# Staggering the first four weight slots of a two-block model kernel by 32 bytes each

## The chip, the core and the metric

One core of a Trainium2 chip runs the whole program. TensorE (PE) multiplies, VectorE (DVE) and ScalarE (ACT) do elementwise work, GpSimd (POOL) does a little of it, and SyncE (SP) issues the weight transfers. The metric is device time in microseconds for one execution. The kernel before takes 2011.96 us, the median of three runs (2011.53 to 2012.35).

## The reference

The input is 256 tokens by 1024 features, batch 1, all in float32. The reference computes one block of a first kind and two of a second, in a row:

```python
def swiglu(y, w_in, w_out):
    a, b = jnp.split(y @ w_in, 2, axis=-1)
    return (jax.nn.silu(a) * b) @ w_out
...
x = ada_out(x, swiglu(ada_in(x, mod, 0, ...), ffn_w_in[l, 0], ffn_w_out[l, 0]), ...)   # also for ctx
# first block: a bidirectional chunked recurrence and a pooling mixer on w_in (1024 x 2064), w_out
x = ada_out(x, swiglu(ada_in(x, mod, 2, ...), ffn_w_in[l, 1], ffn_w_out[l, 1]), ...)
...
for l in range(2):   # second block
    x = x + 0.5 * rms_norm(swiglu_ffn(h, gate, up, down), ...)      # 1024 x 2816 twice, 2816 x 1024
    x = x + rms_norm(hybrid_mixer(h, w_in[l], ...), ...)            # 1024 x 7184, attention, conv, GLA
    x = x + 0.5 * rms_norm(swiglu_ffn(h, gate, up, down), ...)
```

Nearly all arithmetic is products of 256 tokens (512 with the context, in the first block) with large float32 weights. Each weight is read once.

## The kernel before

**Split products.** TensorE's fast float32 form (`float32r`) rounds its operands. So each operand is split into a rounded part and a remainder, hi and lo, and each product is three: hi x hi, hi x lo, lo x hi. In the class Tensor, `product` (L971, L972, L973) streams the weight part as the moving operand, 512 columns, against token parts loaded as stationary weights of the array; in the trace these are `bank<-whi,xTh`, `bank<-wlo,xTh` and `bank<-whi,xTl`, with other token tiles in the place of xTh and xTl. `sub_w` (all through the helper at L935) loads the weight part as stationary and streams 256 tokens: `bank<-xTh,whi` and its like.

**The weight stream.** SP copies a unit of weights (512 KB or 1024 KB) into one of the four raw buffers of `raw`. A unit is cut into sub-units of 128 partitions x 1024 floats. For each sub-unit ACT copies raw to `whi` with rounding (`fill` of Scalar, L1562; L1572 where a gain per row is multiplied in, two instructions of 512 each), then DVE writes raw minus whi to `wlo` (`fill` of Vector, L2191; L2202 with the gain), then TensorE uses both. A slot is one pair whi, wlo, 4096 bytes each per partition. There are 23 slots; slots 0 to 3 are always in the ring, the others borrow memory that is free in some stage (Tables.place deals the slots). All waits between engines are semaphores, and the order on every engine is fixed when the program is written.

**Where the tiles lie.** `Memory.place` gives every tile an address per partition, one after another: raw at 16544, then whi0, wlo0, whi1, ... wlo3, then x, z, junk and the rest. The first address is 160 modulo 256, and nearly all sizes are multiples of 256, so raw, all 23 slots, xTh, xTl, the hidden tiles (hTh, hTl, hwh, hwl), x, z and junk all begin at 160 modulo 256. A few begin elsewhere: modr and brow at 0, yT at 224, sg, qT, kT, mg and tm at 32, gv at 64. uC's rows are 1144 bytes, so its reads begin at many places. Reading through columns of a slot or of xTh moves by multiples of 512 bytes, so an instruction begins where its tile does.

Of the kernel before, what the change touches and what calls it, by code (L numbers as in the profile page):

```python
# [7 lines left out]
F32R = mybir.dt.float32r  # L8
# [83 lines left out]
class Tables:  # L92
# [16 lines left out]
    def place(self):  # L109

        q = len(self.subs)
        s = min(self.ring, key=lambda s: self.guard[s][3] if s in self.guard else -1 if self.holder[s] is None else self.holder[s])
        p, extra = None if s in self.guard else self.holder[s], None
        if s in self.guard:
            kind, key, due, _ = self.guard.pop(s)
            if kind == "spent":
                p = key
            else:
                extra = (kind, key)
            self.due.append(max(self.due[-1] if self.due else 0, due))  # L120
        else:
            self.due.append(max(self.due[-1] if self.due else 0, 0 if p is None else p + 2))
        self.slot.append(s)
        self.before.append((p, extra))
        self.holder[s] = q
        if s in self.once:
            self.ring.remove(s)
            self.once.remove(s)
# [362 lines left out]
class Memory:  # L491
# [47 lines left out]
    def place(self):  # L539
        o = self.low  # L540
        self.raw, o = self.at(o, "raw", [128, NRAW, 2048])
        self.wh, self.wl = [None] * NSPL, [None] * NSPL
        for n in range(4):
            o = self.split_slot(n, o)
        self.x, o = self.at(o, "x", [128, 2, D])
        self.z_at = o
        self.z, o = self.at(o, "z", [128, 2, D])
        self.junk_at = o
        self.junk, o = self.at(o, "junk", [128, D])
        self.ident, o = self.at(o, "ident", [128, 128])  # L550
        self.cols, o = self.at(o, "cols", [128, NCOL + 2])
        self.stats, o = self.at(o, "stats", [128, 24, 8])
        self.fullb, xt = self.at(o, "full", [128, 2, 512])
        self.xTh, o = self.at(xt, "xTh", [128, 8, 256], F32R)
        self.xTl, mid = self.at(o, "xTl", [128, 8, 256], F32R)
        self.bT, o = [], mid
        for n in range(3):
            self.split_slot(4 + n, o)
            if n == 1:
                self.b1_at = o  # L560
            h, o = self.at(o, f"bT{n}h", [128, 4, 256], F32R)
            l, o = self.at(o, f"bT{n}l", [128, 4, 256], F32R)
            self.bT.append((h, l))
        self.xc, o = self.at(xt + 32768, "xc", [128, 2, D])
        self.gp, o = self.at(o, "gp", [128, 2, D])
        self.modc, o = self.at(o, "modc", [128, 3, 2, 2, 8])
        self.gcol, o = self.at(o, "gcol", [128, 3, 2, 8])
        self.selm, o = self.at(o, "selm", [128, 258])
        self.modr, o = self.at(o, "modr", [128, 2, 512])
        self.brow, o = self.at(o, "brow", [128, 2, 512])  # L570
        self.sct, ctx = self.at(o, "sct", [128, 8, 32])
        ctx += (xt - ctx) % 256
        self.place_first(xt, mid, ctx)
        self.place_context(mid)
        self.place_latent(xt, mid)
        gate = xt + 45056
        self.split_slot(7, gate + 4096)
        self.split_slot(8, gate + 12288)
        self.gate, rest = self.at(gate, "gate", [128, 6, 2, 512])
        sil, o = self.at(gate, "silb", [128, 4, 256])  # L580
        self.ffn = {1: self.place_ffn(ctx, "a"), 2: (*self.place_ffn(rest - 4096, "b")[:4], sil)}
        for n, o in ((12, ctx), (15, rest - 4096)):
            self.split_slot(n, o + 2 * HALF_H)
            self.split_slot(n + 1, o)
            self.split_slot(n + 2, o + HALF_H)
        for n in range(5):
            self.split_slot(18 + n, rest + 8192 * n)
        self.place_mixer(rest)

    def split_slot(self, n, o):  # L590
        self.wh[n], o = self.at(o, f"whi{n}", [128, 1024], F32R)
        self.wl[n], o = self.at(o, f"wlo{n}", [128, 1024], F32R)
        return o
    def place_first(self, xt, mid, o):
        self.cTh, c = self.at(mid, "cTh", [128, 8, 256], F32R)
        self.cTl, c = self.at(c, "cTl", [128, 8, 256], F32R)
        assert c == mid + 16384
        self.h = h = o
        self.hwh, o = self.at(o, "hwh", [128, 22, 256], F32R)
        self.hwl, o = self.at(o, "hwl", [128, 22, 256], F32R)  # L600
        self.zc = self.at(o - 8192, "zc", [128, 2, D])[0]
        self.hx, f = self.at(o, "hx", [128, 2, 512])
        self.silx, self.top = self.at(f, "silx", [128, 2, 512])
        self.wh[9], self.wl[9] = self.at(o, "whi9", [128, 1024], F32R)[0], self.at(f, "wlo9", [128, 1024], F32R)[0]
        self.split_slot(10, h)
        self.split_slot(11, h + 22528)

    def place_context(self, mid):

        o = self.top  # L610
        self.vac, o = self.at(o, "vac", [128, 2, 4, 129])
        self.wk, o = self.at(o, "wk", [128, 4, 128])
        self.gb, o = self.at(o, "gb", [64, 2])
        o = mid + 16384
        self.mst, o = self.at(o, "mst", [64, 12])
        self.ones, self.xc_rest = self.at(o, "ones", [64, 128])
        self.uPc, o = self.at(self.xc_rest, "uPc", [128, 4, 258])
        self.g16c, o = self.at(o, "g16c", [128, 256])
        self.Cc, o = self.at(o, "Cc", [128, 2, 64])
        assert o <= mid + 16384 + 8192  # L620
        self.Rc, o = self.at(mid, "Rc", [64, 7, 256])
        self.S0, o = self.at(o, "S0", [128, 8, 129])
        self.S1, o = self.at(o, "S1", [128, 8, 129])
        assert o <= mid + 16384
        self.ktc, o = self.at(self.z_at, "ktc", [128, 2, 512])
        self.uc, o = self.at(o, "uc", [128, 4, 256])
        self.kvc = self.at(self.xc_rest, "kvc", [128, 8, 129])[0]
# [2516 lines left out]
```

How the kernel before makes its waits and increments, by code:

```python
    def __init__(self, m, e):  # L715
        for u, sources in enumerate(m.t.units):
            if u - NRAW in m.t.mod_read:
                nb, half, count = m.t.mod_read[u - NRAW]
                b, n = m.t.bank["mod", nb]
                if half:
                    e.wait_ge(m.full[b], n + 1)
                else:
                    e.wait_ge(m.mod_half, count)
            elif u - NRAW in m.t.part_read:
                e.wait_ge(m.part_done, m.t.part_read[u - NRAW])
            elif u >= NRAW:
                e.wait_ge(m.wlo_done, m.t.subs_through[u - NRAW])
            raw = m.raw[:, u % NRAW, :]
            for part, n, src in sources:
                if part in (0, 1):
                    dst = raw.rearrange("p (k j n) -> p k j n", k=4, j=2)[:, :, part, :]
                else:
                    dst = raw[:, part].rearrange("p (k n) -> p k n", k=n)
                e.dma_start(dst, src).then_inc(m.raw_in[u % NRAW], 16)
        new = 2 * (4 + 2 + 2 + 2 * 6)
        e.wait_ge(m.x_new, new - 2)
        e.dma_start(m.out[0:128, :], m.x[:, 0, :]).then_inc(m.stored, 16)
        for half in range(2):
            c = slice(half * 512, half * 512 + 512)
            e.wait_ge(m.x_new, new - 1 + half)
            e.dma_start(m.out[128:256, c], m.x[:, 1, c]).then_inc(m.stored, 16)
        e.wait_ge(m.stored, 48)
# [5 lines left out]
    def __init__(self, m, e):  # L748
# [25 lines left out]
            if k == 17:  # L774
                e.wait_ge(m.conv1, 8)
                e.wait_ge(m.po_act, 2)
                for n in range(2):
```

## Time and profile before

| | us |
|---|---|
| three runs, median | 2011.96 |
| the profiled execution, its own time | 2011.67 |
| its span, first to last instruction | 2009.5 |
| PE busy in the span | 1978.9 |
| DVE busy | 1343.7 |
| ACT busy | 1106.1 |

The granted TensorE clock is 0.999 of full speed over the span. A matmul's recorded time is longer than the distance to the next one, since two are in the pipeline at once; the distance from start to start is what a product costs.

### The profile page before, as it was taken

How to read it: one execution, taken by the hardware profiler on the slowest of the kernel's cores; microseconds unless marked ns; L12 is line 12 of the kernel's file. 1: busy time of each engine (PE TensorE's matmuls, PEld its weight loads, DVE VectorE, ACT ScalarE, POOL GpSimd, SP SyncE). 2: the span in 40 equal slices, each digit the busy share in tenths (PEclk: the TensorE clock that was granted, in tenths of full speed). 3: DMA queues.
4: the chain of work that ended last, by engine and by line, in shares of the span. 5: the costliest groups of instructions: out<-in, count | busy, mean ns of one | idle time of the engine just before them, and what ended most of it. 6: DMA issues, size and time to landing. Idle time of an engine off the chain costs nothing.

```text
span 2009.5 us, 27521 instructions
## 1 busy us (share of the span) xinstructions
PE 1978.9 (98%) x10838; PEld 1680.9 (84%) x10838; DVE 1343.7 (67%) x2184; ACT 1106.1 (55%) x1746; POOL 70.2 (3%) x139
## 2 busy tenths in 40 slices
PE   7999999999999999999999999999999999999998
PEld 5998899987778888888997888888888897788887
DVE  4457676675887556655688896646665587987653
ACT  4344465445674445554656756545555646766552
POOL 0000000001100000000100000000000200000000
PEclk9999999999999999999999999999999999999999
DMA  9797755675377656555643476555656544367551
GB/s 338 254 303 256 245 190 173 215 255 183 124 233 251 199 195 214 179 196 180 201 147 105 148 238 211 189 168 179 218 174 214 191 126 158 126 203 227 188 185 46
DMA packets 282175, 393.23 MB, mean 196 GB/s; under 512 B 9660, under 2 KB 175996, under 8 KB 282048
## 3 DMA queue, kind: packets, MB, share of 16 engines
q1 hardware_dynamic: 277616, 379.62, 57.5%
q0 software_dynamic: 3456, 9.37, 1.4%
q10 hardware_dynamic: 976, 2.49, 0.3%
q8 instruction: 86, 1.41, 0.3%
q14 instruction: 41, 0.34, 0.1%
HBM read 390.40 MB, written 1.05 MB: 195 GB/s over the span
## 4 chain that ended last, share of the span: by engine, by line
PE 85%; DVE 7%; ACT 3%; DMA 2%; issue 2%; SPq 0%; POOL 0%; DVEq 0%; POOLq 0%; ACTq 0%
PE bank L971 21%; PE bank L973 21%; PE bank L972 21%; PE bank L935 20%; DMA raw<-in_ffn_w_in 2%; DVE wlo L2191 1%; PE bank L1112 1%; DVE junk L2916 1%; PE bank L1020 1%; ACT whi L1562 1%; DMA raw<-in_w_mod 1%; DVE wlo L2202 1%; ACT whi L1572 1%; DVE tm L3073 0%; SPq L734 0%
## 5 line engine op out<-in xcount | busy, mean ns | idle before, releaser
L2191 DVE TENSOR_TENSOR wlo<-raw,whi 128x1024 fp32r<-128x1024 f32 x358 | 433.4, 1224 | 277.0 <-ACT whi L1562 271.2
L1562 ACT ACTIVATE whi<-raw 128x1024 fp32r<-128x1024 f32 x360 | 375.7, 1055 | 376.0 <-PE bank L973 218.0
L971 PE MATMUL bank<-whi,xTh 128*128 128x512 f32 (+1 forms) x1344 | 528.8, 393 | 2.4 <-DVE xTl L2265 2.3
L973 PE MATMUL bank<-whi,xTl 128*128 128x512 f32 (+1 forms) x1344 | 520.7, 387 | 0.0
L972 PE MATMUL bank<-wlo,xTh 128*128 128x512 f32 (+1 forms) x1344 | 520.0, 387 | 0.0
L2202 DVE SCALAR_TENSOR_TENSOR wlo<-raw,cols,whi 128x512 fp32r<-128x512 f32 (+1 forms) x592 | 403.0, 733 | 149.0 <-ACT whi L1572 145.6
L1572 ACT ACTIVATE whi<-raw,cols 128x512 fp32r<-128x512 f32 (+1 forms) x592 | 380.5, 704 | 142.9 <-PE bank L973 108.2
L971 PEld LDWEIGHTS bank<-whi,xTh 128*128 128x128 f32 x1344 | 252.6, 188 | 54.9 <-DVE xTl L2265 3.1
L973 PEld LDWEIGHTS bank<-whi,xTl 128*128 128x128 f32 x1344 | 252.4, 188 | 52.2
L972 PEld LDWEIGHTS bank<-wlo,xTh 128*128 128x128 f32 x1344 | 252.8, 188 | 49.0 <-issue 0.5
L935 PE MATMUL bank<-xTh,whi 128*128 128x256 f32 x696 | 197.0, 284 | 0.0
L935 PE MATMUL bank<-xTl,whi 128*128 128x256 f32 x696 | 195.9, 283 | 0.0
L935 PE MATMUL bank<-xTh,wlo 128*128 128x256 f32 x672 | 190.1, 283 | 0.0
L971 PE MATMUL bank<-whi,hThb 128*128 128x512 f32 x352 | 138.0, 392 | 0.0
L973 PE MATMUL bank<-whi,hTlb 128*128 128x512 f32 x352 | 137.1, 389 | 0.0
L972 PE MATMUL bank<-wlo,hThb 128*128 128x512 f32 x352 | 137.0, 389 | 0.0
L935 PEld LDWEIGHTS bank<-xTh,whi 128*128 128x128 f32 x696 | 133.5, 192 | 1.3 <-issue 1.0
L935 PEld LDWEIGHTS bank<-xTl,whi 128*128 128x128 f32 x696 | 133.5, 192 | 0.4 <-issue 0.2
L935 PEld LDWEIGHTS bank<-xTh,wlo 128*128 128x128 f32 x672 | 128.9, 192 | 0.0
L935 PE MATMUL bank<-cTh,whi 128*128 128x256 f32 x392 | 112.1, 287 | 1.0 <-DVE wlo L2191 0.7
L935 PE MATMUL bank<-cTl,whi 128*128 128x256 f32 x392 | 110.6, 283 | 0.0
L935 PE MATMUL bank<-cTh,wlo 128*128 128x256 f32 x384 | 108.6, 283 | 0.0
(381 smaller groups left out, 2439.2 us busy)
## 6 DMA issues: line engine op xcount, KB each, us to landing
raw<-in_w_in SPq DMA_DIRECT2D x68, 1024.0 KB, 5.1
raw<-in_ffn_w_in SPq DMA_DIRECT2D x132, 512.0 KB, 5.7
raw<-in_ffn_w_gate SPq DMA_DIRECT2D x88, 512.0 KB, 4.1
raw<-in_ffn_w_up SPq DMA_DIRECT2D x88, 512.0 KB, 5.1
raw<-in_ffn_w_down SPq DMA_DIRECT2D x40, 1024.0 KB, 5.0
raw<-in_w_mod SPq DMA_DIRECT2D x36, 1024.0 KB, 6.0
raw<-in_ffn_w_out SPq DMA_DIRECT2D x30, 1024.0 KB, 5.6
raw<-in_w_out SPq DMA_DIRECT2D x12, 1024.0 KB, 5.1
```

Of the source, the lines that this page charges most:

```text
L935: return self.e.matmul(o, lhsT, rhs, start=start, stop=stop, skip_group_check=True)
L971: e.matmul(o, hi[:, kc, sl], wh[:, c], start=at == 0 and k == 0, stop=False)
L972: e.matmul(o, hi[:, kc, sl], wl[:, c], start=False, stop=False)
L973: ins = e.matmul(o, lo[:, kc, sl], wh[:, c], start=False, stop=fin)
L1020: ins = self.e.transpose(bank[:, c * 128:c * 128 + 128], src[:, k * 128:k * 128 + 128], self.m.ident[:, :])
L1112: ins = e.transpose(bank[:, (2 * c + i) * 128:(2 * c + i + 1) * 128], htok[:, 2 * (g % 2) + i, c * 128:c * 128 + 128], m.ident[:, :])
L1562: e.activation(wh, raw, ACT.Copy).then_inc(m.whi_done, 1)
L1572: ins = e.activation(wh[:, c], raw[:, c], ACT.Copy, scale=m.cols[:, a + k:a + k + 1])
L2191: e.tensor_tensor(wl, raw, wh.bitcast(F32), ALU.subtract).then_inc(m.wlo_done, 1)
L2202: ins = e.scalar_tensor_tensor(out=wl[:, c], in0=raw[:, c], scalar=m.cols[:, a + k:a + k + 1], in1=wh[:, c].bitcast(F32), op0=ALU.mult, op ...
L2916: ins = e.scalar_tensor_tensor(out=y[:, c, :], in0=m.uC[:, c, j:j + 256], scalar=w_, in1=y[:, c, :], op0=ALU.mult, op1=ALU.add)
```

## The change

Between whi0 and wlo0, wlo0 and whi1, and so on to wlo3, 32 bytes are left free. So wlo0 begins 32 bytes further on, whi1 64 bytes, and wlo3 224 bytes; modulo 256 the eight parts begin at 160, 192, 224, 0, 32, 64, 96 and 128. x and everything after it lies 256 bytes further on, so that its place modulo 256 is as before. That makes the memory 256 bytes too short at its end, so the small tile gb (two gate biases, 8 bytes per partition) moves from the end into a hole behind sct.

```diff
         for n in range(4):
-            o = self.split_slot(n, o)
+            o = self.split_slot(n, o, 32)
...
-        self.sct, ctx = self.at(o, "sct", [128, 8, 32])
+        self.sct, o = self.at(o, "sct", [128, 8, 32])
+        self.gb, ctx = self.at(o, "gb", [64, 2])
         ctx += (xt - ctx) % 256
...
-    def split_slot(self, n, o):
+    def split_slot(self, n, o, gap=0):
         self.wh[n], o = self.at(o, f"whi{n}", [128, 1024], F32R)
-        self.wl[n], o = self.at(o, f"wlo{n}", [128, 1024], F32R)
-        return o
+        self.wl[n], o = self.at(o + gap, f"wlo{n}", [128, 1024], F32R)
+        return o + gap
...
         self.wk, o = self.at(o, "wk", [128, 4, 128])
-        self.gb, o = self.at(o, "gb", [64, 2])
```

No instruction is added, removed or moved: on each of the five engines the order, the operands' names and the semaphores are the same. Only the line numbers differ: from L613 on a line is numbered two higher, so L971 becomes L973, L1562 becomes L1564 and L2191 becomes L2193.

Of the 9448 product matmuls of the program, counted in its list of instructions, 6460 read slots 0 to 3: 3612 with 512 moving columns and 2848 with 256. ACT has 968 rounding instructions and DVE as many for the remainders; 607 of each write slots 0 to 3.

## Rows read from the trace of the kernel before

**Rows 1.** The page: busy us (share of the span) x instructions, by engine.
```profile
PE 1978.9 (98%) x10838; PEld 1680.9 (84%) x10838; DVE 1343.7 (67%) x2184; ACT 1106.1 (55%) x1746; POOL 70.2 (3%) x139
```

**Rows 2.** Waits of PE: engine, line, releaser: us in total, times, longest us.
```profile
PE bank L935 <- DMA raw<-in_w_mod: 11.5, 3, 6.9
...
PE bank L935 <- DVE wlo L2191: 0.7, 2, 0.4
```

**Rows 3.** The page: lines' shares of the chain that ended last.
```profile
PE bank L971 21%; PE bank L973 21%; PE bank L972 21%; PE bank L935 20%; DMA raw<-in_ffn_w_in 2%; DVE wlo L2191 1%; PE bank L1112 1%; DVE junk L2916 1%; PE bank L1020 1%; ACT whi L1562 1%; DMA raw<-in_w_mod 1%; DVE wlo L2202 1%; ACT whi L1572 1%; DVE tm L3073 0%; SPq L734 0%
```

**Rows 4.** The chain in order of time: start us, us, what (longest pieces).
```profile
277.76 1.75 PE bank L1020 x16
...
351.37 51.59 PE bank L935 x432
976.15 46.07 PE bank L935 x384
```

**Rows 5.** Windows: stretch, length, busy us of PE, PEld, DVE, ACT, POOL; clock, DMA.
```profile
1022.22:1033.13 10.91, 10.91 (x51) 9.02 (x50) 10.91 (x32) 7.75 (x20) 0.00 (x0) 1.00 0.35 104
829.94:834.02 4.08, 4.08 (x19) 3.38 (x19) 1.82 (x3) 2.32 (x4) 0.00 (x0) 1.00 0.78 240
```

**Rows 6.** Windows, the same columns: two groups of an FFN.
```profile
834.30:857.02 22.72, 22.72 (x105) 18.81 (x104) 14.01 (x24) 13.12 (x22) 0.00 (x0) 1.00 0.58 186
```

**Rows 7.** Timeline of PE, mixer: start us, us, instruction; junk begins at 160.
```profile
1115.22 1.89 PE L935 MATMUL bank<-junk,stk 128*128 128x256 f32 x8
1116.76 0.58 PE L971 MATMUL bank<-whi,xTh 128*128 128x512 f32 x1
```

**Rows 8.** Timeline of PE, same mixer: sg begins at 32.
```profile
1128.74 1.89 PE L935 MATMUL bank<-sg,stk 128*128 128x256 f32 x8
1130.27 0.58 PE L971 MATMUL bank<-whi,xTh 128*128 128x512 f32 x1
```

**Rows 9.** Timeline of PE, x8 transposes of x (160), then slower products.
```profile
1205.67 1.04 PE L1020 MATMUL bank<-ident,x 128*128 128x128 f32 x8
1206.46 0.47 PE L971 MATMUL bank<-whi,xTh 128*128 128x512 f32 x1
...
1207.00 0.40 PE L973 MATMUL bank<-whi,xTl 128*128 128x512 f32 x1
...
1208.39 0.40 PE L973 MATMUL bank<-whi,xTl 128*128 128x512 f32 x1
```

**Rows 10.** Timeline of PE, x8 transposes of mg (32).
```profile
1797.90 1.04 PE L1497 MATMUL bank<-ident,mg 128*128 128x128 f32 x8
1798.69 0.48 PE L971 MATMUL bank<-whi,xTh 128*128 128x512 f32 x1
```

**Rows 11.** Groups by shape: line, instruction, count; busy us, mean ns; idle before.
```profile
L2191 DVE TENSOR_TENSOR wlo<-raw,whi 128x1024 fp32r<-128x1024 f32 x358 | 433.4, 1224 | 277.0 <-ACT whi L1562 271.2 <-POOL stats L855 3.7
L1562 ACT ACTIVATE whi<-raw 128x1024 fp32r<-128x1024 f32 x358 | 374.5, 1058 | 373.9 <-PE bank L973 215.9 <-PE bank L935 85.2 <-DMA raw<-in_ffn_w_in 57.7
L2202 DVE SCALAR_TENSOR_TENSOR wlo<-raw,cols,whi 128x512 fp32r<-128x512 f32 x560 | 389.6, 747 | 145.1 <-ACT whi L1572 141.7
```

**Rows 12.** Instructions of L2265: ns min/median/max, first and last start us.
```profile
L2265 DVE TENSOR_TENSOR hwl<-hx,hwh x22: 683/684/693, 57.3 to 405.2; 128x512 fp32r<-128x512 f32 x22
L2265 DVE TENSOR_TENSOR xTl<-yT,xTh x2: 671/672/672, 543.6 to 545.0; 128x512 fp32r<-128x512 f32 x2
```

**Rows 13.** Instructions on the tiles modr, mg and junk, the same columns.
```profile
L2359 DVE SCALAR_TENSOR_TENSOR modr<-raw,sct,modr x42: 743/752/755, 174.2 to 653.8; 128x512 f32<-128x512 f32 x42
L3075 DVE TENSOR_TENSOR mg<-mg,tm x16: 691/692/694, 1160.1 to 1795.9; 128x512 f32<-128x512 f32 x16
L2110 ACT ACTIVATE sg<-junk x2: 1061/1062/1064, 1121.5 to 1740.0; 128x1024 f32<-128x1024 f32 x2
```

**Rows 14.** Instructions on the tile gb: the DMA, and ns of one reader.
```profile
L2634 DVE TENSOR_SCALAR Rx<-bank,gb x2: 466/469/472, 501.3 to 502.3; 32x256 f32<-32x256 f32 x2
L762 POOL DMA_DIRECT2D gb<-in_gate_b x1: 552/552/552, 160.2 to 160.2; - x1
```

## The prediction

> **What bounds the kernel now.** I read the busy shares first. PE is busy 1978.9 of 2009.5 us, 98%, with DVE at 67% and ACT at 55% [rows 1]. The page warns that a busy PE is not a PE at its peak, so I went on to PE's own waits. The longest is for a DMA at the very start, 11.5 us; for the remainders (wlo), which the changed addresses touch, PE stood still 0.7 us in the whole span [rows 2]. The chain of waits says the same: the three 512-column products have 21% each and the 256-column ones 20%, together 83%; the two kinds of remainder instruction and the two kinds of rounding come to about 1% each [rows 3]. So the kernel is as long as TensorE's stream of products, and the change can move the time only if it changes the distance between two products, or makes a product wait for a rounded or a remainder part.
>
> Next I took that distance in stretches of one kind. 432 products with 256 columns take 51.59 us and 384 others 46.07 us: 0.119 and 0.120 us each [rows 4]. With 512 columns, 18 starts lie in 4.08 us, 0.2267 us each, while DVE is busy less than half and ACT a little more than half of the stretch. In another stretch, where DVE is busy the whole time and ACT for 7.75 of 10.91 us, 48 starts lie in 10.91 us, 0.2273 us each [rows 5]. (The counts in those rows include the matmuls cut by the edges.) At the granted clock 1.00, which is the 2.4 GHz level, 512 columns are 0.2133 us, so 0.013 us of each product is something else.
>
> **The change, part by part.**
>
> *The products themselves.* 6460 of 9448 product matmuls read slots 0 to 3. Before, the streamed operand and the loaded one both begin at 160 modulo 256. Afterwards the distance between the two is one of eight values, from 0 to 224. The question is whether a matmul, or a matmul beside DVE and ACT, notices that. The trace has no split product with unequal beginnings, so I take the nearest rows. Eight matmuls of 256 columns stream junk, which begins at 160; the next instruction starts 1.54 us after them [rows 7]. Eight of the same form in the same mixer stream sg, which begins at 32, against the same small matrix: 1.53 us [rows 8]. That is 0.192 us for each, whether the beginning is 160 or 32. Eight transposes of x (160) take 0.79 us to the next start and eight of mg (32) also 0.79 us [rows 9, 10]. In both pairs the difference is under 0.01 us in eight, about 1 ns for one. The value is 0. The bounds from the same rows are 1 ns either way, for 6460 products 6.5 us. That is the last digit of the view filled to its edge, so I allow half of it, 3.2 us, for this term.
>
> *The products beside DVE and ACT.* If three engines at the same place modulo 256 got in each other's way, it would show where they overlap. It shows 0.6 ns (0.2273 against 0.2267) between the stretch where DVE never rests and the one where it mostly does [rows 5]. For 3612 products with 512 columns in slots 0 to 3 that is at most 2.2 us, if the whole of it were a matter of beginnings and the stagger removed all of it. I take 0: the engines move through their operands at different rates, so where each begins says little about where they stand against each other a moment later.
>
> *Remainders and rounding.* DVE reads raw and whi and writes wlo in step, one element each at a time, so here a common beginning could count. A remainder takes 1224 ns and a rounding 1058 ns for 1024 elements, one with a gain 747 ns for 512 [rows 11]. For unequal beginnings there are rows: the same subtraction of 512 elements takes 684 ns in the middle with all three tiles at 160, and 672 ns with the source (yT) at 224 [rows 12], 12 ns or 1.8% less. The scalar-tensor form with raw at 160 and its other input and its output (modr) at 0, just as a staggered slot would stand, takes 752 ns, 5 ns more than the 747; the sum of two tiles at 32 takes 692 ns, 8 ns or 1.2% more than 684; and ACT from junk (160) to sg (32) takes 1062 ns against 1058 [rows 11 to 13]. So one instruction changes by between -1.8% and +1.2%, and the row that is nearest to a staggered slot says +0.7%. These four kinds hold about 4% of the chain, 80 us [rows 3], and 607 of 968 of them are in the slots concerned: 50 us of the path, so -0.9 to +0.6 us. I take 0, since the rows of both signs are equally near. Off the path a few nanoseconds do nothing: DVE waited 271 us for ACT's rounding [rows 11], and TensorE's 0.7 us is all that it waited for DVE in turn. If that cover were gone, all 607 would count, at 5 ns each 3 us.
>
> *The rest.* x, z, xTh and all later tiles move by 256 bytes and keep their place modulo 256: 0. gb moves, is loaded once by one small DMA, and is read by eight DVE instructions of about 470 ns [rows 14]: at most a few ns each, 0. raw doesn't move, so no weight transfer changes its target. No instruction, wait or queue entry changes, so nothing is queued behind anything new.
>
> The sum is 2011.67 us (the profiled execution, 2009.5 of it the span) + 0 + 0 + 0 = 2011.7 us. The median of the three runs is 0.29 us higher, 2011.96. I forecast 2011.9 us. The allowances, 3.2, 2.2 and 0.9 us, seldom add up; together they make about 3 us each way.
>
> **A rule weighed.** Rows 5 say 0.6 ns between a crowded and a less crowded stretch. The Trainium skill, in "SBUF — State Buffer", section "A bandwidth-pool intuition that's wrong (but worth ruling out)", says that the memory is multi-ported and that contention on it is structural, a lock on a port or a starved descriptor generator, and no sharing of one bandwidth; the section "Door 1: The DMA port swizzle" of the same page puts the banks that the compute engines see in groups of partitions, not in addresses along a partition. By that rule the stagger has nothing to act on, and the sum is exactly that of before; the trace agrees to within the 0.6 ns that it leaves.
>
> **The rivals.**
>
> *Faster: collisions of address go away.* Two groups of a feed-forward stage take 22.72 us for 96 products and 8 transposes [rows 6]. 96 x 0.2267 is 21.76 us, and 8 transposes at 1.75/16 = 0.109 us [rows 4] are 0.88 us, together 22.64. Some 0.08 us, 0.35%, is left, and one sees it as products at longer distances: from 1207.00 to 1208.39 us six take 1.39 us, 0.232 us each, 5 ns more than the usual [rows 9]. If that excess were collisions of equal beginnings throughout, it would be 0.35% of 2009.5 us, 7.1 us, and the share of slots 0 to 3 is 6460/9448 of it, 4.8 us: 2007.1 us. For it: the excess exists, and everything stands at 160 now. Against it: it lies in the few products after transposes, and the busiest stretch for DVE lacks it [rows 5]. A larger form would attack the 13 ns that a product takes over its columns; 6460 times that is 84 us, for which only the number speaks, since it is the same for the streams of 256 and of 512 columns and looks like a fixed cost of changing the stationary operand.
>
> *Slower: the stagger makes collisions.* It could be that equal beginnings are the good case for TensorE's two reads, since the streamed and the loaded operand then keep a fixed distance, and that some of the seven new distances make them meet. The place is the 512-column stream on slots 0 to 3, the price the one slow distance that the trace knows, 5 ns [rows 9]: 3612 x 5 ns = 18 us, 2030 us; if half of the distances do it, 9 us, 2021 us. It decides from 1.1 ns per product (4 us / 3612). For it: no product of the trace has unequal beginnings. Against it: junk against sg, and x against mg, show no difference for such a pair [rows 7 to 10].
>
> *The change doesn't do what it says.* The places modulo 256 do change for the eight parts, but if the memory is divided in larger steps than 256 bytes, or in partitions alone, then the beginnings meet or miss each other as before. It gives 2012 us like the forecast; what would tell it apart is that not even DVE's remainders change by a nanosecond.
>
> **How the numbers follow.** A measurement of this kernel can tell about 0.2% from no change, 4 us. No effect that can be told, for whichever of the two reasons: 0.84 (0.60 the forecast, 0.24 the third rival). Faster by collisions that go away: 0.09, at 2007 us. Slower by collisions made: 0.07, at 2021 to 2030 us. The forecast's own range is 2009 to 2015 us. I let the low end reach 2008, towards the faster rival, and the high end 2015, and leave the slower rival out with most of its 0.07 and the faster with about half of its 0.09.
>
> **What the profile of the changed kernel would show.** The stretches of 432 and 384 products should again take 51.6 and 46.1 us, and the 512-column products 0.227 us from start to start; the means of the remainder and rounding lines should stay within 1224 +- 22 and 1058 +- 10 ns. If the distances in the two groups of a feed-forward stage fall to 22.64 us from 22.72, the faster rival is right; if they rise, the slower. The forecast is wrong if DVE's remainder in slots 0 to 3 differs from that in other slots by more than 2%, or if the time moves by over 4 us.

## The result and the profile after

The changed kernel takes 2023.79 us (median of three runs, 2023.41 to 2025.20) against 2011.96 before. The ratio is 1.006, with a 95% interval from 1.0046 to 1.0074: slower by 0.6%, 11.8 us, where no change was forecast. In its profiled execution the span is 2023.0 us against 2009.5, 13.5 us more; that execution was the longest of the three, 1.4 us above the median. (From L613 on, the profile after numbers a line of before one higher, not two as said ahead: L971 is now L972.)

The page after, busy shares [rows 1 before]:

```profile
PE 1991.5 (98%) x10838; PEld 1675.4 (83%) x10838; DVE 1343.8 (66%) x2184; ACT 1106.7 (55%) x1746; POOL 69.4 (3%) x139
```

DVE and ACT do the same work in the same time (+0.1 and +0.6 us). PE is busy 12.6 us longer with the same 10838 matmuls, and idle 31.5 us against 30.6: the loss is in the matmuls. The waits of PE [rows 2 before] hardly grew:

```profile
PE bank L936 <- DMA raw<-in_w_mod: 12.7, 4, 7.0
...
PE bank L936 <- DVE wlo L2192: 1.2, 2, 0.7
```

The groups by shape show that neither the remainders nor the roundings noticed the stagger: their means are 1224, 746 and 1058 ns now and were 1224, 747 and 1058 [rows 11]. Taken by slot, a remainder of 1024 elements takes 1222 to 1228 ns in slots 0 to 3 both before and after, and 1224 in the others. What changed are the products; the first row is from before, the others from after.

```profile
L971 PE MATMUL bank<-whi,xTh 128*128 128x512 f32 x1312 | 519.7, 396 | 2.4 <-DVE xTl L2265 2.3
...
L972 PE MATMUL bank<-whi,xTh 128*128 128x512 f32 x1312 | 523.2, 399 | 2.4 <-DVE xTl L2266 2.3
...
L2192 DVE TENSOR_TENSOR wlo<-raw,whi 128x1024 fp32r<-128x1024 f32 x358 | 433.5, 1224 | 279.0 <-ACT whi L1563 273.2 <-POOL stats L856 3.7
L2203 DVE SCALAR_TENSOR_TENSOR wlo<-raw,cols,whi 128x512 fp32r<-128x512 f32 x560 | 389.3, 746 | 148.9 <-ACT whi L1573 146.6
L1563 ACT ACTIVATE whi<-raw 128x1024 fp32r<-128x1024 f32 x358 | 374.6, 1058 | 378.5 <-PE bank L974 223.9 <-PE bank L936 82.1 <-DMA raw<-in_ffn_w_in 57.4
```

The chain in order of time, its pure stretches of 256-column products [rows 4 before]:

```profile
351.49 50.94 PE bank L936 x432
...
981.86 45.74 PE bank L936 x384
```

These are shorter than before: 432 products take 50.94 us and not 51.59, 384 take 45.74 and not 46.07. But the second begins at 981.86 us instead of 976.15: between the end of the one and the start of the other, where nearly all products have 512 columns, 579.4 us pass and not 573.2, 6.2 us more. PE's timeline shows where. These are the transposes that end a group of the second feed-forward stage, in the kernel before, and then after; from the first row of a fence to the second lie two groups, 96 products and 8 transposes:

```profile
834.77 0.60 PE L1112 MATMUL bank<-ident,htokb 128*128 128x128 f32 x4
857.49 0.60 PE L1112 MATMUL bank<-ident,htokb 128*128 128x128 f32 x4
```

```profile
838.96 0.60 PE L1113 MATMUL bank<-ident,htokb 128*128 128x128 f32 x4
861.87 0.60 PE L1113 MATMUL bank<-ident,htokb 128*128 128x128 f32 x4
```

That is 22.72 us before and 22.91 after, 2.0 ns more for each of the 96 products in the mean. By slot, 36 of them read slots 0 to 3 and take 0.17 us of it, 4.7 ns each; the other 60 take 0.01 us, and the 8 transposes are as before.

Each of the 9448 product matmuls of the trace can be matched with its slot, since the order is fixed. The mean distance from one start to the next of the same kind, waits left out, is then:

| | before, ns | after, ns | products | us |
|---|---|---|---|---|
| 512 columns, slots 0 to 3 | 227.2 | 232.0 | 3612 | +17.3 |
| 512 columns, other slots | 227.2 | 227.8 | 2508 | +1.5 |
| 256 columns, slots 0 to 3 | 119.9 | 118.1 | 2848 | -5.1 |
| 256 columns, other slots | 120.0 | 119.9 | 480 | 0 |

The sum is +13.7 us, against 13.5 us of the spans. What the table leaves out nearly cancels: pairing the two traces matmul by matmul, waits between products took about 2 us more, and the stretches with float32 matmuls and transposes about 1.5 us less. So the loss is in TensorE's own distance between products, and two effects of opposite sign are in it.

### The profile page after: what moved, and what is told of

Its sections match the earlier page's. It is cut to its first block, busy times and chain, and to the rows that moved or that the text cites. A ratio compares the mean times of both kernels' runs of the same rounds, so it can differ in the third digit from the quotient of the medians.

```text
span 2023.0 us, 27521 instructions
## 1 busy us (share of the span) xinstructions
PE 1991.5 (98%) x10838; PEld 1675.4 (83%) x10838; DVE 1343.8 (66%) x2184; ACT 1106.7 (55%) x1746; POOL 69.4 (3%) x139
## 4 chain that ended last, share of the span: by engine, by line
PE 85%; DVE 5%; issue 3%; ACT 2%; DMA 2%; POOL 0%; SPq 0%; DVEq 0%; POOLq 0%; ACTq 0%
PE bank L972 22%; PE bank L973 22%; PE bank L974 22%; PE bank L936 18%; DMA raw<-in_ffn_w_in 2%; PE bank L1113 1%; DVE junk L2917 1%; PE bank L1021 1%; DVE wlo L2203 1%; ACT whi L1573 1%; DVE wlo L2192 0%; ACT whi L1563 0%; ACT junk L1628 0%; DMA pm<-in_pool 0%; DVE Sg L3016 0%
## 5 line engine op out<-in xcount | busy, mean ns | idle before, releaser
L2192 DVE TENSOR_TENSOR wlo<-raw,whi 128x1024 fp32r<-128x1024 f32 x358 | 433.5, 1224 | 279.0 <-ACT whi L1563 273.2
L972 PE MATMUL bank<-whi,xTh 128*128 128x512 f32 (+1 forms) x1344 | 532.2, 396 | 2.4 <-DVE xTl L2266 2.3
L973 PE MATMUL bank<-wlo,xTh 128*128 128x512 f32 (+1 forms) x1344 | 524.3, 390 | 0.0
L972 PEld LDWEIGHTS bank<-whi,xTh 128*128 128x128 f32 x1344 | 252.5, 188 | 58.8 <-DVE xTl L2266 3.2
L973 PEld LDWEIGHTS bank<-wlo,xTh 128*128 128x128 f32 x1344 | 252.7, 188 | 51.1 <-issue 0.5
L972 PE MATMUL bank<-whi,hThb 128*128 128x512 f32 x352 | 139.0, 395 | 0.0
L973 PE MATMUL bank<-wlo,hThb 128*128 128x512 f32 x352 | 138.1, 392 | 0.0
```

Source lines behind the costliest of these rows:

```text
L972: e.matmul(o, hi[:, kc, sl], wh[:, c], start=at == 0 and k == 0, stop=False)
L973: e.matmul(o, hi[:, kc, sl], wl[:, c], start=False, stop=False)
L2192: e.tensor_tensor(wl, raw, wh.bitcast(F32), ALU.subtract).then_inc(m.wlo_done, 1)
```

## The experiments

The theories before the first four runs: **A**, the streamed and the loaded operand of one matmul get in each other's way by the distance of their beginnings modulo 256; **B**, the jump from one streamed operand to the next costs; **C**, the shift of later tiles or of gb; **D**, collisions with DVE and ACT.

**e1_distances.** A kernel of its own, TensorE alone at work:

```diff
+for width in (512, 256):
+    for j in E8:          # loaded tile begins at 32 * j
+        for i in E8:      # streamed tile begins at 32 * i
+            run(30, [(mov[i], sta[j])], width)
+# then, for each i: part, part 32 bytes on, part, against one loaded tile, x48
+# (with 256 columns the loaded tile changes and the streamed one stays)
```

> This kernel computes none of the reference; it only multiplies, with no other engine at work meanwhile, and writes zeros. Eight streamed tiles (mova to movh) begin at 0, 32, ... 224 modulo 256, eight loaded ones (staa to stah) likewise; each of the 64 pairs runs 30 times with 512 and 30 times with 256 columns, then eight patterns of three as in the products (part, part 32 bytes on, part). Theory A (TensorE's two reads get in each other's way by the distance of their beginnings modulo 256): equal pairs at 227 and 120 ns from start to start as in the kernel before; unequal ones differ by pair, with 512 columns 1 to 9 ns more, with 256 columns 1 to 4 ns less, and all pairs of one distance are alike. Theory B (a jump from one streamed operand to the next costs): all 64 pairs alike at 227 and 120 ns, and only the patterns of three differ. Theory D (the collisions are with VectorE and ScalarE): nothing here differs.

PE's timeline, streamed tiles mova to movh against the loaded tile staf (at 160); a row is 30 matmuls, and the distance to the next row's start is what they take. With 512 columns:

```profile
402.81 7.16 PE L59 MATMUL bank<-mova,staf 128*128 128x512 f32 x30
409.81 7.13 PE L59 MATMUL bank<-movb,staf 128*128 128x512 f32 x30
...
430.81 7.16 PE L59 MATMUL bank<-move,staf 128*128 128x512 f32 x30
437.81 6.99 PE L59 MATMUL bank<-movf,staf 128*128 128x512 f32 x30
444.63 7.16 PE L59 MATMUL bank<-movg,staf 128*128 128x512 f32 x30
451.63 7.03 PE L59 MATMUL bank<-movh,staf 128*128 128x512 f32 x30
```

With 256 columns:

```profile
718.85 3.69 PE L59 MATMUL bank<-movc,staf 128*128 128x256 f32 x30
722.37 3.57 PE L59 MATMUL bank<-movd,staf 128*128 128x256 f32 x30
725.78 3.71 PE L59 MATMUL bank<-move,staf 128*128 128x256 f32 x30
729.33 3.75 PE L59 MATMUL bank<-movf,staf 128*128 128x256 f32 x30
732.91 3.70 PE L59 MATMUL bank<-movg,staf 128*128 128x256 f32 x30
```

With equal beginnings (movf, staf) 30 products of 512 columns take 6.82 us, 227 ns each; with most others 7.00 us, 233 ns. With 256 columns the equal pair is the slow one: 3.58 us, 119 ns, while movd, 64 bytes before the loaded tile, takes 3.41 us, 114 ns. All eight equal pairs agree, and so do pairs of one distance elsewhere in the two 8 x 8 tables, to about 1 ns. So the distance decides, not the address. One distance is an exception and has two settled values: with 256 columns and 192 bytes, five of eight pairs run at 113.3 ns and three at 117.8. The most frequent settled means, in ns from start to start:

| streamed minus loaded, mod 256 | 0 | 32 | 64 | 96 | 128 | 160 | 192 | 224 |
|---|---|---|---|---|---|---|---|---|
| 512 columns | 226.7 | 233.3 | 228.9 | 233.6 | 233.3 | 234.4 | 233.3 | 233.3 |
| 256 columns | 119.9 | 117.8 | 117.8 | 119.8 | 118.7 | 117.4 | 113.3 | 118.3 |

Theory A is borne out, and D isn't needed for the effect: nothing but TensorE was at work. B fails as the whole story, since single pairs without any jump differ. The patterns of three that slots 0 to 3 now have take 231.7, 231.1, 229.2 and 231.2 ns (48 products each), 230.8 in the mean, 4.1 ns over the equal pair. But the prices of single pairs don't add up to these: by the table the first pattern (distances 0, 32, 0) should take 228.9 ns and takes 231.7, the third (128, 160, 128) should take 233.7 and takes 229.2. So the order of distances counts too, and how is not shown.

**e2_shift_only.** Everything of the change but the stagger:

```diff
-            o = self.split_slot(n, o, 32)
+            o = self.split_slot(n, o)
+        o += 256
```

> All of the change but the stagger: the eight parts of slots 0 to 3 begin at 160 modulo 256 as before, the 256 bytes are left free behind them in one piece, and gb lies in its new place. Theories A, B and D: 2012 us, as before, within 2 us. Theory C (what lies 256 bytes further on, or gb, costs the time): 2024 us.

Measured 2011.72 us against 2012.14 before, ratio 0.9999 (0.9989 to 1.0008). The chain has the stretches of before to 0.01 us:

```profile
350.96 51.59 PE bank L937 x432
976.25 46.07 PE bank L937 x384
```

Theory C is out: the shift and gb's new place cost nothing that these runs can tell, 2 us at most.

**e3_lo_only.**

```diff
-            o = self.split_slot(n, o, 32)
+            self.wh[n], o = self.at(o, f"whi{n}", [128, 1024], F32R)
+        o += 32
+        for n in range(4):
+            self.wl[n], o = self.at(o, f"wlo{n}", [128, 1024], F32R)
+        o += 224
```

> The four rounded parts at 160 modulo 256 as before, the four remainders at 192. Theory A: the remainder's products are at distance 32 (232 ns with 512 columns, 118 with 256), the others, two of three, at 0; so about a third to two thirds of the 12 us: 2015 to 2020 us. Theory B (the jump of 32 bytes between whi and wlo): all of it, 2024 us. Theory C: 2024 us.

Measured 2023.24 us, ratio 1.0055 (1.0040 to 1.0070): 11.1 us, nearly the whole loss, more than A's expectation. One remainder at a distance makes its two neighbours slow too. Over all products with 512 columns in slots 0 to 3 the mean from start to start is 231.9 ns; by kind it is 231.7 from hi x hi to the remainder's product, 234.4 from that one to the next, and 229.5 from there. The pattern 160, 192, 160 had given 231.7 in e1. I had priced each product by its own pair alone, and that is too little. A hint lies in the trace of e1: the load for a matmul starts 2 to 5 ns after the start of the matmul before it, so the two reads that overlap in time belong to neighbours. Whether that is why the neighbours pay was not tried. Taken alone this run would have spoken for B.

**e4_pairs.**

```diff
-            o = self.split_slot(n, o, 32)
+            o = self.split_slot(n, o) + 64
```

> whi and wlo of one slot begin at the same place, the slots at 160, 224, 32 and 96 modulo 256. Theory A: three of four slots at a distance, with 512 columns 2709 products by 3 to 5 ns, less 2136 products of 256 columns by 1 to 2 ns: 2016 to 2022 us. Theory B (the jump between the parts of a slot): 2012 us, since a slot has no jump inside. Theory C: 2024 us.

Measured 2020.45 us, ratio 1.0042 (1.0028 to 1.0056), inside A's range. B wanted 2012: it falls, since no slot has a jump inside here. That a jump adds something of its own, on top of the distance, is not excluded by this.

**e5_group64 and e6_group128.** No stagger, but all eight parts at one distance from the tokens, 64 or 128:

```diff
+        o += 64                 # e6: 128
         for n in range(4):
-            o = self.split_slot(n, o, 32)
+            o = self.split_slot(n, o)
+        o += 192                # e6: 128
```

> All eight parts of slots 0 to 3 begin 64 bytes further on modulo 256 (224, the tokens at 160), no stagger among them. Theory A, priced by the map of the distances (with 512 columns the streamed part 64 ahead of the loaded tokens: 228.9 against 226.7 ns; with 256 columns the loaded part 64 ahead of the streamed tokens: 113.3 against 119.9 ns): 3612 x 2.2 = +7.9 us, 2848 x 6.6 = -18.8 us, so 2001 us. Rival E (any distance other than 0 costs, as the three slower kernels did): 2020 us or more.

> The same with 128 bytes in the place of 64. Theory A by the map (233.3 against 226.7 ns, and 118.7 against 119.9 ns): 3612 x 6.6 = +23.8 us, 2848 x 1.2 = -3.4 us, so 2032 us, the slowest of all. Rival E: as the changed kernel, 2024 us, and no further from e5 than a few us.

Measured: e5 2009.09 us, ratio 0.9988 (0.9980 to 0.9997); e6 2027.16 us, ratio 1.0079 (1.0065 to 1.0092), both against 2011.6. The order is as the map says, and the same move by 64 or by 128 bytes gives a gain or the slowest kernel of all; rival E is out. But the sizes are smaller: -2.5 and +15.6 us where -10.9 and +20.4 were expected. By the slots of the trace, e5's products of 256 columns went from 119.9 to 114.7 ns, not to 113.3, and those of 512 columns to 229.6 in slots 0 to 3 and to 228.1 in the others, where the map has 228.9 and 226.7. In e6 the 512-column products in slots 0 to 3 are at 232.6, not 233.3. The kernel changes its token chunk and its slot all the time, and the map was read from settled streams. That is my reading of the shortfall, argued and not tried: in the maps a stream needs some four to ten products to settle, and in e1 the fast distance of 192 did not always reach its faster value; in e5 a fifth of the 256-column products in slots 0 to 3 are at 118 ns or more. Waits between products grew by 2.5 us in e5 as well.

**e7_tokens and e8_context_tokens.** The slots stay at 160; tokens move to 96, in e7 xTh, xTl, cTh and cTl, in e8 only the last two:

```diff
-        self.xTh, o = self.at(xt, "xTh", [128, 8, 256], F32R)
-        self.xTl, mid = self.at(o, "xTl", [128, 8, 256], F32R)
+        self.xTh, o = self.at(xt + 192, "xTh", [128, 8, 256], F32R)    # e7 alone
+        self.xTl, o = self.at(o, "xTl", [128, 8, 256], F32R)
+        xt += 256
+        mid = o + 64                                                   # e8: o + 256
...
-        self.cTh, c = self.at(mid, "cTh", [128, 8, 256], F32R)
+        self.cTh, c = self.at(mid - 64, "cTh", [128, 8, 256], F32R)    # both
```

> The slots stay at 160; the token tiles xTh, xTl, cTh and cTl begin at 96, so that every product of them with a slot is at the good distance of 64, while the hidden tiles and the branch tiles, whose products have 512 columns, stay at 0. Theory A by the map: all 3232 products with 256 columns and loaded slots by 6.6 ns less, -21.3 us; 3984 with 512 columns on x and c tokens by 2.2 ns more, +8.8 us; 1999 to 2000 us. Rival E: over 2020 us.

> Only cTh and cTl begin at 96, all else at 160. Theory A by the map: 1168 products with 256 columns by 6.6 ns, 7.7 us less; 48 with 512 columns cost 0.1: 2004.5 us. If the opening stage is held by its weight transfers, a part of it is lost: 2004 to 2009 us. Rival E: 2012 us or more.

Measured: e7 2002.89 us, ratio 0.9954 (0.9942 to 0.9967), faster than both kernels, by 8.7 us than the one before; e8 2008.69 us, ratio 0.9980 (0.9972 to 0.9989). The chain of e7:

```profile
295.86 47.41 PE bank L939 x404
343.54 49.20 PE bank L939 x432
```

432 products of 256 columns take 49.20 us, 114 ns each, against 51.59 [rows 4]. In e8 the stretches on context tokens are shorter, while those on xTh are as before. The first row is from before, the other two from e8; the 240 matmuls are 216 products on context tokens and 24 of another kind:

```profile
148.07 31.64 PE bank L935 x240
...
146.76 30.33 PE bank L938 x240
...
348.13 51.59 PE bank L938 x432
```

The direction is as expected in both, the size again about two thirds of the map in e7 and less than half in e8 (2.9 us of 7.7). That is 6 ns less for each of the 216. The trace of e8 shows where its shortfall lies. The 256-column products on context tokens went from 120.0 to 114.4 ns, which is 6.4 us of the 7.7; but PE then waited 2.7 us longer between products. So a part of what the products gained went into waits, which the expectation's upper end had allowed for.

**e9_fine_map.** As e1, in steps of 16 bytes, and past 256:

```diff
+AWAY = [16 * i for i in range(16)] + [320, 1088]    # mova .. movp, movq, movr
+for width in (512, 256, 384, 128):
+    for t in mov:
+        run(60, [(t, sta)], width)
```

> This kernel computes none of the reference; TensorE alone at work, one loaded tile, eighteen streamed tiles, 0 to 240 bytes behind it in steps of 16 modulo 256, and then 320 and 1088, each 60 times with 512, 256, 384 and 128 columns. Theory A with a period of 256 bytes: 320 and 1088 (both 64 modulo 256) cost what 64 does, 228.9 and 117.8 ns. If the period were 512 or more, they would differ from it. Steps of 16 that share a multiple of 32 are alike if the unit is 32 bytes, and in between or different if it is 16.

PE's timeline, 60 matmuls a row; move is 64 bytes behind sta, movq 320, movr 1088:

```profile
167.73 13.91 PE L60 MATMUL bank<-move,sta 128*128 128x512 f32 x60
181.47 14.02 PE L60 MATMUL bank<-movf,sta 128*128 128x512 f32 x60
...
334.87 13.91 PE L60 MATMUL bank<-movq,sta 128*128 128x512 f32 x60
348.62 13.90 PE L60 MATMUL bank<-movr,sta 128*128 128x512 f32 x60
362.35 7.36 PE L60 MATMUL bank<-mova,sta 128*128 128x256 f32 x60
...
685.19 6.86 PE L60 MATMUL bank<-movb,sta 128*128 128x128 f32 x60
691.89 6.87 PE L60 MATMUL bank<-movc,sta 128*128 128x128 f32 x60
```

64, 320 and 1088 take 13.74, 13.75 and 13.73 us for 60: the period is 256 bytes. Steps of 16 matter: settled, 512 columns take 226.7, 231.6 and 233.3 ns at distances 0, 16 and 32, and again 226.7 at 240. With 256 columns 112 is as good as 192, 113.3 ns. With 384 columns it is 173.3 to 180.0, with 128 columns always 111.7 ns.

**e10_float32.** The form of the rows on which the forecast stood, alone:

```diff
-        sta = at(..., "sta", 2048)
+        sta = at(..., "sta", 2048, F32)      # and the streamed tiles
```

> As the map of distances, but with plain float32 tiles, the form of junk, sg and the transposes, in the place of float32r; computes none of the reference. Eight distances in steps of 32 bytes, 60 matmuls each with 256 and with 128 columns. Theory A with the addition that the plain form is held by something slower than the two reads (its rows in the kernel before showed 192 ns at two different beginnings): all distances within 0.5 ns of each other. Without the addition: differences of 1 to 7 ns as in float32r, and the two rows of the kernel before agreed by chance.

The timeline; the trace has two records for each plain float32 matmul:

```profile
208.19 26.06 PE L60 MATMUL bank<-movb,sta 128*128 128x256 f32 x120
234.09 26.06 PE L60 MATMUL bank<-movc,sta 128*128 128x256 f32 x120
259.99 26.06 PE L60 MATMUL bank<-movd,sta 128*128 128x256 f32 x120
285.89 26.06 PE L60 MATMUL bank<-move,sta 128*128 128x256 f32 x120
...
363.59 26.06 PE L60 MATMUL bank<-movh,sta 128*128 128x256 f32 x120
389.49 13.56 PE L60 MATMUL bank<-mova,sta 128*128 128x128 f32 x120
```

All distances from 32 to 224 take 25.90 us to the hundredth, and with 128 columns 13.40. Distance 0 stands in one row with the opening stream; by its records it takes the same, 215.8 ns for a record with 256 columns. The plain form doesn't notice the distance at all; why was not tried.

## Why the prediction was wrong, point by point

*What bounds the kernel* was right: TensorE's stream of products, and the sum of the distances between its starts gives the 13.5 us of the span.

*The products themselves* is the step that failed. It put the term at 0, from "the nearest rows": junk against sg [rows 7, 8] and the transposes of x against those of mg [rows 9, 10]. None of those four rows is float32r: two are plain float32 matmuls, two are transposes of float32 tiles. e10 shows the plain matmul deaf to the very thing that moves the float32r one by up to 8 ns (e1); the form of the transposes was not run alone. The rows were near by size and by place, and not by the property in question. The pair of rows 7 and 8 was misread besides: the kernel has four matmuls there and the trace two records for each, so 1.54 us is 0.38 us a matmul and not 0.192, and a difference of 0.01 us in four bounds one of them by 2.5 ns and not 1. Over 6460 products that is 16 us, more than the whole loss. The allowance drawn from these rows was too narrow: measured +4.8 ns for 512 columns in slots 0 to 3 and -1.8 ns for 256. I had noted that "the trace has no split product with unequal beginnings"; a term with no row of its own form, over 6460 products, should have had the range of its rivals.

*The products beside DVE and ACT*: 0 was right. e1 shows the effect with both at rest, and in the trace after, the 512-column products in slots 0 to 3 take 231.9 ns both where neither engine is at work (175 of them) and where both are (1045); before it was 226.8 and 227.6. The argument that engines at different rates don't keep in step fits this between engines. Inside TensorE it doesn't hold: the streamed and the loaded operand begin in the same relation each time a product repeats, and the small difference comes back in all 6460.

*Remainders and rounding* at 0 was right: the means are as before, in slots 0 to 3 too. *The rest* at 0 was right (e2).

*The rule weighed*: the Trainium skill's "SBUF — State Buffer" ("A bandwidth-pool intuition that's wrong (but worth ruling out)" and "Door 1: The DMA port swizzle") gave no effect of addresses along a partition. The runs disagree for TensorE's two reads in float32r, by 6.6 ns in 226.7; the measurement decides. The Trainium skill's "TensorE: Matmul & The Clock Gate", section "Step-by-step: what each phase is for", speaks of two independent read ports, one for the streamed and one for the loaded operand; by these timings the two are not independent in this form.

*The slower rival* had the mechanism: the stagger makes the two reads meet, on the 512-column stream of slots 0 to 3, at 5 ns a product, "3612 x 5 ns = 18 us". Measured there: 4.8 ns, 17.3 us. It lacked the other sign, 5.1 us gained on the 256-column products, and 1.5 us on products in other slots, and it got 0.07. That its price of 5 ns came out so well is partly luck: it was taken from the slow products behind a transpose, which all begin at equal places. Its "Against it" were the same four rows. *The faster rival* took the 13 ns over the columns for a fixed cost of changing the loaded operand; with 256 columns e1 finds half of it gone at distance 192 (119.9 to 113.3 ns), so a part of it is not fixed.

## What to carry to other kernels

Where TensorE's float32r products bound a kernel, place the streamed and the loaded tile by their distance modulo 256 bytes: equal beginnings for 512 columns, and for 256 columns the streamed one 64 bytes before the loaded one; then measure, since the real order of tiles gave between a quarter and three quarters of what settled streams promise (e5 to e8). The two wishes can conflict, as here, where the weights are the streamed operand in one kind of product and the loaded one in the other. When a term is bounded by "the nearest row", ask whether the row has the operand type and form of the thing, and if it hasn't, measure it alone in a small kernel first: one such kernel with 64 pairs in two widths settled here what three variants of the whole kernel (e2 to e4) could only hint at.

## What the hardware showed unexpectedly

The settled distances in float32r often are multiples of 6.67 ns: 113.3, 120.0, 173.3, 180.0, 226.7, 233.3, which is 16 columns at the granted 2.4 GHz. Values in between, such as 228.9 at distance 64, are means of a repeating pattern of shorter and longer ones (from 225 to 232 ns in e9), and a mean on such a step can be one too: 231, 231 and 238 ns at distance 96. With 128 columns the mean, 111.7 ns, is no such multiple. 256 columns can go in 113.3 ns and 512 never took less than 226.7 in a settled stream, so the cost over the columns is 6.7 and 13.3 ns at best. Why for 512 columns a distance of 240 is harmless and one of 64 nearly so (2.2 ns), while 32 costs 6.6 ns, stays open: the experiments show the period, that steps of 16 bytes count, and the sign for each width, and not the circuit.
